# Two output tiles side by side in the linear blocks of a two-model transformer kernel

## The reference

```python
u = rms_norm(h, norm_g)
z = u @ w_in
...
h = h + jnp.concatenate([oa, ob], axis=-1) @ w_out
gate = jax.nn.sigmoid(rms_norm(h, ple_norm_g) @ w_ple_gate)
return h + (p_i @ w_ple) * gate
```

```python
x = x + 0.5 * swiglu(rmsnorm(x, ffn1_norm[l]), ffn1_w1[l], ffn1_w3[l], ffn1_w2[l])
...
x = x + jnp.concatenate([o_a, o_b], axis=-1) @ w_out[l]
x = x + mem_cross_attention(rmsnorm(x, xa_norm[l]), rmsnorm(mem, mem_norm[l]), xa_wq[l], xa_wkv[l], xa_wo[l])
x = x + 0.5 * swiglu(rmsnorm(x, ffn2_norm[l]), ffn2_w1[l], ffn2_w3[l], ffn2_w2[l])
```

## Time and profile before

| what | value |
|---|---|
| median of three runs | 3361.12 us |
| span of the profiled execution | 3377.2 us |
| TensorE matmul busy | 3210.1 us (95%), 18864 matmuls and as many weight loads |
| VectorE, ScalarE, GpSimd busy | 1494.4, 1093.0, 60.1 us |
| mean granted TensorE clock | 0.963 |
| DMA | 80 GB/s over the span |

### The profile page before, as it was taken

One profiled execution on the slowest core, in us unless ns is written; L12 is line 12 of the kernel. 1 busy time (PEld: TensorE's weight loads), 2 busy tenths in 40 slices (PEclk: granted clock), 3 DMA queues, 4 the chain that ended last, 5 costly groups with the idle time before them and its releaser, 6 DMA issues. The chain is left out here.

```text
span 3377.2 us, 44214 instructions
## 1 busy us (share of the span) xinstructions
PE 3210.1 (95%) x18864; PEld 2834.3 (84%) x18864; DVE 1494.4 (44%) x1752; ACT 1093.0 (32%) x1321; POOL 60.1 (2%) x68
## 2 busy tenths in 40 slices
PE   7999989999979999999999999899999989999998
PEld 7998879898968887988888888788889888888886
DVE  3454443454434445535344444444446353434444
ACT  3433333433332223432333222322225323432222
POOL 0000000000000000010000000000000110000000
PEclk8997998997989999989999999999999999999999
DMA  3111112120222222301322222222223112322222
GB/s 119 64 63 38 59 68 71 39 88 5 71 97 100 97 97 85 120 13 63 105 82 87 89 98 98 77 99 99 87 99 109 42 51 75 107 81 100 90 98 79
DMA packets 41263, 270.99 MB, mean 80 GB/s; under 512 B 6272, under 2 KB 6528, under 8 KB 10016
## 3 DMA queue, kind: packets, MB, share of 16 engines
q1 hardware_dynamic: 41120, 268.99, 22.6%
HBM read 266.81 MB, written 2.10 MB: 80 GB/s over the span
## 5 line engine op out<-in xcount | busy, mean ns | idle before, releaser
L173 DVE TENSOR_TENSOR w_lo<-w_raw,w_hi 128x2048 fp32r<-128x2048 f32 x242 | 554.1, 2290 | 454.1 <-ACT w_hi L167 453.4
L185 PE MATMUL PS<-w_hi,uh 128*128 128x256 f32 x2560 | 734.5, 287 | 12.4 <-DVE ul L329 6.6
L186 PE MATMUL PS<-w_lo,uh 128*128 128x256 f32 x2560 | 727.1, 284 | 0.0
L187 PE MATMUL PS<-w_hi,ul 128*128 128x256 f32 x2560 | 726.9, 284 | 0.0
L167 ACT ACTIVATE w_hi<-w_raw 128x2048 fp32r<-128x2048 f32 x242 | 462.9, 1913 | 637.2 <-PE PS L187 633.3
L185 PE MATMUL PS<-uh,w_hi 128*128 128x512 f32 x1600 | 623.1, 389 | 5.5 <-DVE ul L329 5.5
L186 PE MATMUL PS<-ul,w_hi 128*128 128x512 f32 x1600 | 622.5, 389 | 0.0
L187 PE MATMUL PS<-uh,w_lo 128*128 128x512 f32 x1600 | 622.5, 389 | 0.0
L185 PEld LDWEIGHTS PS<-w_hi,uh 128*128 128x128 f32 x2560 | 494.1, 193 | 24.6 <-issue 15.2
L186 PEld LDWEIGHTS PS<-w_lo,uh 128*128 128x128 f32 x2560 | 494.4, 193 | 1.0 <-issue 1.0
L187 PEld LDWEIGHTS PS<-w_hi,ul 128*128 128x128 f32 x2560 | 494.1, 193 | 0.0
(11 more groups left out here) (280 smaller groups left out, 3219.1 us busy)
## 6 DMA issues: line engine op xcount, KB each, us to landing
w_raw<-in_w SPq DMA_DIRECT2D x242, 1024.0 KB, 4.8
X<-in_x SPq DMA_DIRECT2D x1, 2048.0 KB, 10.1
memory<-in_mem SPq DMA_DIRECT2D x2, 1024.0 KB, 5.0
out<-X SPq DMA_DIRECT2D x4, 512.0 KB, 2.8
bands<-in_bands SPq DMA_DIRECT2D x2, 768.0 KB, 6.0
mask_numbers<-in_masks SPq DMA_DIRECT2D x1, 1152.0 KB, 6.3
p_raw<-in_pT SPq DMA_DIRECT2D x2, 512.0 KB, 6.4
lb<-in_lb_logits SPq DMA_DIRECT2D x2, 512.0 KB, 3.3
```

Source lines behind the costliest of these rows:

```text
L173: dve.tensor_tensor(self.lo[g % 2][:], self.raw[g % 2][:], self.hi[g % 2][:], ALU.subtract).then_inc(self.lo_done, 1)
L185: pe.matmul(out, sh, mh, start=first, stop=False)
L186: pe.matmul(out, sh, ml, start=False, stop=False)
L187: return pe.matmul(out, sl, mh, start=False, stop=last)
```

## The change

Where two output tiles of a block can be worked on together, their three products alternate: first high with high of both, then high with low of both, then low with high of both. The number, shapes and operands of all matmuls stay as they are.

```diff
+def side_by_side(pe, pair, first, last):
+    for out, (sh, sl), (mh, ml) in pair:
+        pe.matmul(out, sh, mh, start=first, stop=False)
+    for out, (sh, sl), (mh, ml) in pair:
+        pe.matmul(out, sh, ml, start=False, stop=False)
+    return [pe.matmul(out, sl, mh, start=False, stop=last) for out, (sh, sl), (mh, ml) in pair]
 def block_to_tokens(pe, w, g, u, outs, nt=NT, kd=KD, halves=1, before=None, made=None,
                     tile_done=None):
...
     if made:
-        n = BLK // KD
         for k in range(KD):
-            for t in range(nt):
+            for t in range(0, nt, 2):
                 if t == 0 or k == 0:
-                    made(pe, k, t + 1)
-                last = split_products(
...
+                    made(pe, k, t + 2)
+                done = side_by_side(pe, [one(t, 0, k), one(t + 1, 0, k)], k == 0, k == KD - 1)
...
+    for t in range(0, nt, 2):
         if before:
             before(t)
...
+            before(t + 1)
+        for k in range(kd):
+            done = side_by_side(pe, [one(t, 0, k), one(t + 1, 0, k)], k == 0, k == kd - 1)
+        if tile_done:
+            done[0].then_inc(tile_done, 1)
+            if t < nt - 2:
+                done[1].then_inc(tile_done, 1)
+    done[1].then_inc(w.used, 1)
 def block_to_features(pe, w, g, u, outs, made=None, first_done=None):
...
+    if first_done:
+        for f in range(2):
+            for k in range(KD):
+                last = split_products(pe, *one(f, k), k == 0, k == KD - 1)
...
+    for k in range(KD):
+        if made:
+            made(pe, k, 2)
+        done = side_by_side(pe, [one(0, k), one(1, k)], k == 0, k == KD - 1)
+    done[1].then_inc(w.used, 1)
...
         def down_part(g, t, k):
-            for half in range(2):
...
+            return side_by_side(pe, [
+                (PS[:, 4 + 2 * (t % 2) + half, :], [x[:, k, t * P:(t + 1) * P] for x in (f.h_hi, f.h_lo)],
+                 [x[g % 2][:, k * D + half * 512:k * D + half * 512 + 512] for x in (w.hi, w.lo)]) for half in range(2)],
+                k == 0, k == 1)[1]
```

More of the change, by code:

```diff
@@ L187, in split_products, with one @@
     return pe.matmul(out, sl, mh, start=False, stop=last)
+def side_by_side(pe, pair, first, last):
[4 more added lines that the diff above has]
+    return [pe.matmul(out, sl, mh, start=False, stop=last) for out, (sh, sl), (mh, ml) in pair]
 def block_to_tokens(pe, w, g, u, outs, nt=NT, kd=KD, halves=1, before=None, made=None,
                     tile_done=None):
+    n = BLK // kd // halves
+    def one(t, h, k):
+        a = k * n * halves + h * n
+        return (outs(t, h), [x[:, k, t * P:(t + 1) * P] for x in u],
+                (w.hi[g % 2][:, a:a + n], w.lo[g % 2][:, a:a + n]))
@@ L196, in block_to_tokens @@
     if made:
-        n = BLK // KD
         for k in range(KD):
-            for t in range(nt):
+            for t in range(0, nt, 2):
                 if t == 0 or k == 0:
-                    made(pe, k, t + 1)
-                last = split_products(
-                    pe, outs(t, 0), [x[:, k, t * P:(t + 1) * P] for x in u],
-                    (w.hi[g % 2][:, k * n:(k + 1) * n], w.lo[g % 2][:, k * n:(k + 1) * n]), k == 0, k == KD - 1)
-        last.then_inc(w.used, 1)
-        return
-    n = BLK // kd // halves
@@ L208, in block_to_tokens @@
-    for t in range(nt):
+                    made(pe, k, t + 2)
+                done = side_by_side(pe, [one(t, 0, k), one(t + 1, 0, k)], k == 0, k == KD - 1)
+        done[1].then_inc(w.used, 1)
+        return
+    if halves == 2:
+        for t in range(nt):
+            for k in range(kd):
+                done = side_by_side(pe, [one(t, 0, k), one(t, 1, k)], k == 0, k == kd - 1)
+            if tile_done and t < nt - 1:
+                done[1].then_inc(tile_done, 1)
+        done[1].then_inc(w.used, 1)
+        return
@@ L275, in block_to_features, with one @@
 def block_to_features(pe, w, g, u, outs, made=None, first_done=None):
-    for f, k in [(f, k) for k in range(KD) for f in range(2)] if made else [(f, k) for f in range(2) for k in range(KD)]:
-        if made and (f == 0 or k == 0):
-            made(pe, k, f + 1)
+    def one(f, k):
         a = k * 256 + f * P
[L282 to L287, removed]
+        return outs(f), (w.hi[g % 2][:, a:a + P], w.lo[g % 2][:, a:a + P]), [x[:, k, :] for x in u]
+    if first_done:
+        for f in range(2):
+            for k in range(KD):
+                last = split_products(pe, *one(f, k), k == 0, k == KD - 1)
+            if f == 0:
+                last.then_inc(first_done, 1)
+        last.then_inc(w.used, 1)
+        return
+    for k in range(KD):
+        if made:
+            made(pe, k, 2)
+        done = side_by_side(pe, [one(0, k), one(1, k)], k == 0, k == KD - 1)
+    done[1].then_inc(w.used, 1)
 def to_features_phase(block, sem, name, PS, ident, src, nt, uh, ul, gain=None, norm=None, alone=False, extra=None,
```

## The result

The changed kernel takes **3389.9 us** (median of five runs, 3376.9 to 3402.1) beside 3361.4 us for the kernel before (median of five, 3351.6 to 3370.9). The ratio is 1.0087, with a 95% interval of 1.0062 to 1.0112: 21 to 38 us slower. The forecast was 3382 us in a range of 3360 to 3396. The profiled execution of the changed kernel took 3402.1 us with a span of 3400.2, 23.0 us above the span of before.

A forecast was written before the change was run, and what follows sets the result against it. TensorE, busy for 95% of the span, was taken to bound the kernel; -2.4 + 10.4 + 4.0 + 3.6 + 5 = +20.6 us on the median of 3361.1 gave 3382 us, range 3360 to 3396.

The forecast's parts named there:

- The distance of matmuls: Time between matmul starts in token and feature blocks, claimed to stay at 0.120 and 0.2267 us: 0 us.
- Down blocks -2.4 us: In down blocks, half of the extra 0.0023 us on 2112 matmuls was claimed to go: -2.4 us.
- The tails: Ends of `out1`, `out2`, `xout`: tile 2 ends later, so scaling comes 1.59, 1.59 and 2.01 us later; two layers, +10.4 us.
- E: Start of the last matmul of an output projection's last block, from which the forecast timed the operations behind it.
- The starts: Phase starts wait for later slices of `ul`: +4.0 us at 6 feature starts, +3.6 us at 10 token starts.
- The wait moved in `projection_phase_1`: Wait ahead of tile 3 moves ahead of tile 2, 2.88 us sooner; taken as 0, at most 2.88 us per layer.
- The clock: Longer idle time ahead of the transposes at `out2` and `xout` was claimed to bring the 1.2 GHz clock: +5 us.
- four borders: The transposes behind `out2` and `xout` in two layers, the only places counted for a lower clock: 0 to 8.2 us.
- The rival of a wider fall (+16): All six tails and the first matmuls behind them at 1.2 GHz: +16 instead of +5, 3393 us; chance 0.05.
- The rival of the bank: Accumulating into one bank stalls fp32r products; alternating gains up to 150 us, giving 3232 us; chance 0.12.
- The bounds: Stated sum of the terms' lower and upper ends, some 12 to 29 us, used for the case's own range 3368 to 3396.
- the upper bound for token blocks: Upper end for the starts of token blocks, given as 12 x 0.67 us; both kinds of starts together 0 to +12.

The follow-up runs named there:

- e3: Changed kernel with the old order of products in blocks that count `tile_done` and in the first block of each phase: 3366.9 us, ratio 1.0015 to the kernel before.
- m1_banks: Separate kernel of only rows of 96 matmuls, varying bank, stationary tile, columns and type: fp32r with 512 columns 0.2267 us each in two and eight banks.
- e5: Changed kernel, but in blocks that count `tile_done` only tiles 0 and 1 are paired, tiles 2 and 3 computed one after the other: 3364.3 us, ratio 1.0011.
- e1: Kernel before, with pairing only in the blocks that count `tile_done`: 3379.7 us, ratio 1.0059.
- e4: Kernel before with its own order of products, but the changed waits for slices of `ul`: 3363.4 us, ratio 1.0017.
- e8: Changed kernel with 9 or 14 unread filler products behind the last block of each output projection: 3380.5 us, ratio 1.0051 to the kernel before.
- e2: Kernel before, with pairing and its waits only in the first block of a phase, which waits for slices of `ul`: 3370.6 us, ratio 1.0022.
- e9: Changed kernel as it is, run again on the same chip as the version with filler products: 3390.2 us, ratio 1.0086 to the kernel before.
- e7: Kernel before, with k as outer loop over all four tiles in blocks that count `tile_done`, so all end late: 3380.4 us, one execution.

## Why the prediction was right

- *The distance of matmuls is unchanged.* Right, and shown three ways: the changed kernel, e3, and m1_banks. The argument from the rows of before (a third of the steps changed bank already and were no shorter) was enough.
- *Down blocks -2.4 us.* Wrong, a small term. The step that failed is "half of the steps there will now be between two like products, so I take half": the distance stayed at 0.2289, so the new order took nothing of the extra 0.0023.
- *The tails.* The mechanism was right and the size within 0.4 us of 10.4. The add of tile 3 came at E + 1.77 instead of E + 1.90, since VectorE starts it before the reciprocal has run out, and the scaling in `xout` at E + 3.44 instead of 3.37. The three tails measured 10.1 us. e5 takes the whole term away by the order of tiles 2 and 3 alone, e1 brings it alone.
- *The starts.* Right in mechanism and size: 3.7 for features, 3.6 for tokens. e4 shows them without any pair. Their effect on the time of the whole kernel was too small for its interval.
- *The wait moved in `projection_phase_1`* was costed at 0; inside that phase TensorE has no idle time over 0.22 us ahead of a projection product behind the first block's start, before or after. It wasn't tried alone.
- *The clock.* +5 was the least founded term, and it measured 8.5. The four borders measured 3.9 us, close to it, but two places were missing: `ple` of layer 2 (+1.6), ahead of which TensorE's idle time grew from 0.73 us to 2.16, and the start of the gate (+3.0), where the clock fell at four of the six starts of three profiles (the changed kernel, the same again, and e8). The step that failed was to count "four borders" where six tails and the waits at the starts had become longer. The rival of a wider fall (+16) was nearer in place than in size.
- *The other side.* The rival of the bank needed 0.0015 us a matmul to outweigh the rest; the rows show token and feature matmuls unchanged to the last digit, 0.120 and 0.2267, and down matmuls 0.2289 for 0.2290.
- *The bounds.* "Some 12 to 29 us" doesn't come out of the ends named for the terms; they add up to 5.5 at the lower end (-4.9 + 10.4) and 35.5 at the upper (4.9 + 10.4 + 12 + 8.2), without the projection. The 12 starts of the upper bound for token blocks should be the 10 that the term counts.

The measured 3389.9 us lie in the forecast's range. The measured sum in the trace (+26) is above the forecast's +20.6 by 2.4 of the down term and 3.5 of the clock, less 0.6 of the tails and the starts. The clock's part is in some measure luck: the gate's 3.0 us came in one trace of the changed kernel and half of them in the other.

The Trainium skill (TensorE: Matmul & The Clock Gate, Back-to-back issue gap) gives N / 2.4 + 2.5 ns for a warm, isolated matmul. m1_banks agrees for bf16 (109.2 ns at 256 columns, the rule gives 109.2) and disagrees for fp32r (120.0 and 226.7 ns, the rule 109.2 and 215.8). The same page (A second HAM failure mode: psum-queue depth-cycling) reports a clock that swings in a kernel that goes round the banks, and puts it down to short idle times between groups of matmuls. The rows here, which have no such idle times, don't show it: with eight banks in turn m1_banks has 0.2267 us a matmul, and the token blocks of the changed kernel 0.120.

## What to carry to other kernels

When a change reorders a bound engine's work, look first at the trace of before for places that already have the new order; if their distance is the same, expect nothing of the order itself, and what remains is when each output is finished and when each input is needed. Two outputs side by side finish together: every consumer that worked on the first while the second was computed moves behind the end of the block, and at a border with a serial chain (add, square, mean, root, scale) that is paid once per border (1.43 to 2.08 us here). Where there is no such reader, pairing cost nothing that could be measured here and gained nothing (e3); where there is one, leave the last two outputs of a block one after the other (e5).

## What the runs showed that was not expected

**fp32r has an extra of its own.** 0.0133 us beyond the columns at 256 and at 512 columns, whatever the bank; bf16 has 0.0025 at 256 columns, and a float32 record of 256 columns takes 0.2158 us, 0.0025 above two passes. It is 11% of each token matmul of this kernel, and no order of the matmuls tried here touches it. Whether it is the product or the load of its weights isn't shown.

**The scatter between executions lies in whole stages that run at either clock.** The kernel before ran between 3347 and 3382 us in 29 executions on one chip. Stretches of PE over the attention stages of the first model's two layers (busy, count, PEclk, DMA share, GB/s), first in the kernel before, then in e2:

```profile
297.00:360.00 63.00, 58.89 (x286) 0.70 0.00 1
764.00:828.00 64.00, 60.55 (x292) 0.70 0.00 1
```

```profile
304.00:351.70 47.70, 43.59 (x294) 1.00 0.00 1
756.00:802.70 46.70, 42.59 (x291) 1.00 0.00 1
```

The same work takes some 63 us at a mean clock of 0.70, or some 47 at 1.00: 16 us each, more than the price of all six tails. The same code does it too: the second attention of layer 1, from the last projection product ahead of it to its own last product, took 64.5 us in the first profile of the changed kernel and 53.2 in the second (e9), and the spans are 10 us apart. So the profiled execution of e2 has a span of 3348.8, 28 us under the span of before, although e2 does more waiting, and its median is not lower. Spans of single executions of this kernel can't be compared; stages with the same clock can, and medians of a dozen runs.

**A short extra wait can cost the clock after it.** Over all traces with these gaps, 2.17 us from the last matmul to the transposes were followed by transposes at 1.2 GHz at 2 of 20 borders (the kernel before, e2 to e5), 3.49 to 4.25 us at 14 of 16 (the changed kernel twice, e1, e7). Ahead of `ple` it was 6 of 8 after 2.28 to 2.44 us and none after 1.01. With fillers in the gap (e8) none of the four borders and neither `ple` was slow. So the longer wait makes the lower clock likely, not certain.
